# Both FFNs' end in a Trainium2 trunk layer: three tiles scaled between the last operands, the shift of four tiles moved to TensorE

## The reference, cut to what matters

```python
h = modulate(rms_normalize(x), sh1, sc1)              # h*(1+scale)+shift
x = x + 0.5 * gt1 * swiglu(h, w_ffn1_in, w_ffn1_out)  # first FFN, hidden 2816
h = modulate(rms_normalize(x), sh2, sc2)              # <- made at the end of the first FFN
y = hybrid_mixer(h, ...)
x = x + gt2 * y
h = modulate(rms_normalize(x), sh3, sc3)
x = x + 0.5 * gt3 * swiglu(h, w_ffn2_in, w_ffn2_out)  # second FFN
return rms_normalize(x) * g_final                     # <- made at the end of the second FFN
```

## Time and profile before

| | |
|---|---|
| median of 3 runs | 1986.99 us (1985.71 to 1988.73) |
| the profiled execution, its own time | 1988.55 us |
| its span in the profile, first to last instruction | 1986.8 us (1.75 us lie around it) |
| mean granted TensorE clock | 0.985 |
| end of the first FFN (last item to the barrier) | 705 to 735 us of the span |
| end of the second FFN | 1965 to 1987 us of the span |

### The profile page before, as it was taken

The page is one execution under the profiler, slowest core; times in us unless marked ns, Lnnn a source line. Parts: engine busy times, 40 slices in busy tenths (PEclk is TensorE's granted clock), DMA queues, the critical chain, the costliest instruction groups (busy, mean ns, idle before and its releaser), DMA issues. The chain is left out here.

```text
span 1986.8 us, 25496 instructions
## 1 busy us (share of the span) xinstructions
PE 1908.7 (96%) x9368; PEld 1568.6 (79%) x9368; DVE 1163.5 (59%) x1696; ACT 756.8 (38%) x1382; POOL 835.3 (42%) x612
## 2 busy tenths in 40 slices
PE   6989999999999989999999998998999999999997
PEld 6878888888888867777778887776888888888886
DVE  5876666654777771454514556568345344458777
ACT  4542223232444532554513444244333332334444
POOL 1597887674000111000011241398788778700002
PEclk7999999999999989999999999999999999999999
DMA  9155666633975300311112112513232233168652
GB/s 339 58 192 182 191 190 197 189 117 117 370 239 192 107 22 25 125 44 43 64 33 69 51 35 85 205 71 122 85 128 96 95 113 103 58 226 338 203 190 85
DMA packets 208107, 267.94 MB, mean 135 GB/s; under 512 B 14302, under 2 KB 125170, under 8 KB 206450
## 3 DMA queue, kind: packets, MB, share of 16 engines
q1 hardware_dynamic: 207986, 266.34, 40.0%
HBM read 211.16 MB, written 53.03 MB: 133 GB/s over the span
## 5 line engine op out<-in xcount | busy, mean ns | idle before, releaser
L446 POOL TENSOR_TENSOR ffn_ring_b<-ffn_raw_in,ffn_ring_b 128x512 fp32r<-128x512 f32 x156 | 222.9, 1437 | 113.6 <-ACT ffn_ring_b L441 113.6
L1052 PE MATMUL bank<-ffn_w_hi,ffn_a_hi 128*128 128x512 f32 x616 | 240.0, 390 | 1.2 <-DVE ffn_w_lo L1036 1.2
L1054 PE MATMUL bank<-ffn_w_hi,ffn_a_lo 128*128 128x512 f32 x616 | 239.7, 389 | 0.0
L1053 PE MATMUL bank<-ffn_w_lo,ffn_a_hi 128*128 128x512 f32 x616 | 239.6, 389 | 0.0
L1803 POOL TENSOR_TENSOR mx_w_lo<-mx_raw_w,mx_w_hi 128x1024 fp32r<-128x1024 f32 x26 | 62.7, 2421 | 357.5 <-ACT mx_w_hi L1606 290.7
L109 POOL TENSOR_SCALAR rms<-rms 128x1 f32<-128x1 f32 x24 | 13.3, 555 | 469.7 <-ACT ffn_junk L103 455.1
L441 ACT CAST ffn_ring_b<-ffn_raw_in 128x512 fp32r<-128x512 f32 x160 | 99.2, 622 | 267.4 <-PE bank L1504 255.6
L1025 ACT CAST ffn_a_hi<-ffn_a_stage 128x512 fp32r<-128x512 f32 x154 | 95.6, 621 | 200.4 <-PE bank L1054 196.0
L1319 DVE TENSOR_TENSOR ffn_u<-bank,ffn_u 128x512 f32<-128x512 f32 x106 | 72.9, 688 | 158.0 <-PE bank L1504 157.9
L1036 DVE TENSOR_TENSOR ffn_a_lo<-ffn_a_stage,ffn_a_hi 128x512 fp32r<-128x512 f32 x154 | 106.4, 691 | 73.6 <-ACT ffn_a_hi L1025 73.5
L446 POOL TENSOR_TENSOR ffn_ring_a_lo<-ffn_raw_in,ffn_ring_a_hi 128x512 fp32r<-128x512 f32 x96 | 132.2, 1388 | 31.9 <-ACT ffn_ring_a_hi L441 29.9
(11 more groups left out here) (379 smaller groups left out, 4750.2 us busy)
## 6 DMA issues: line engine op xcount, KB each, us to landing
ffn_raw_in<-in_w_ffn_in SPq DMA_DIRECT2D x88, 512.0 KB, 5.9
ffn_a_stage<-hidden SPq DMA_DIRECT2D x154, 256.0 KB, 3.7
ffn_w_stage<-in_w_ffn_out SPq DMA_DIRECT2D x132, 256.0 KB, 3.4
ada_rest<-in_w_ada SPq DMA_DIRECT2D x64, 448.0 KB, 3.9
hidden<-ffn_u SPq DMA_DIRECT2D x88, 256.0 KB, 2.0
hidden<-ffn_g SPq DMA_DIRECT2D x66, 256.0 KB, 2.0
mx_raw_w<-in_w_mix_in SPq DMA_DIRECT2D x28, 512.0 KB, 4.2
xres<-in_x SPq DMA_DIRECT2D x16, 512.0 KB, 8.7
```

What stands on the lines that cost most here:

```text
L446: pool.tensor_tensor(self.lo(q), self.source(b, m), self.hi(q).bitcast(F32), ALU.subtract)\
L1052: pe.matmul(dst, a_hi, w_hi, start=first, stop=False, skip_group_check=True)
L1053: pe.matmul(dst, a_hi, w_lo, start=False, stop=False, skip_group_check=True)
L1054: mm = pe.matmul(dst, a_lo, w_hi, start=False, stop=True, skip_group_check=True)
```

## The change

- In both FFNs ScalarE's `square` of tiles 0 to 3 comes after items 70 to 73 instead of 71 to 74.
- In both FFNs VectorE scales tiles 0, 1 and 2 between the items, behind items 72, 73 and 74, and tile 3 after the last item.
- First FFN: VectorE adds the shift to tiles 0 to 3 alone. Tiles 4 to 7 are transposed unshifted, and TensorE adds the shift in PSUM: for each of the two banks of a tile two more matmuls of 512 columns, with the shift's high and low part (4 rows of 128) as one operand and a 4 x 512 pattern of ones and zeros as the other. For that the shift is also loaded as rows (4 x 2 x 128); ScalarE makes their high part and the pattern behind item 70 (`rows_hi`), and VectorE their low part after the last item (`rows_lo`).
- First FFN: the 128 x 1024 shift has another place in memory, so its load moves from item 44 to a point after all items' loads, behind a wait for the low parts of item 68.
- Second FFN: `scale_out(4)` comes behind the last `add` instead of ahead of it.

```diff
@@ class Norm
+    def rows_hi(self, act):
+        act.wait_ge(self.loaded, 32)
+        act.copy(self.rows["hi"], self.rows["raw"]).then_inc(self.rows_done, 1)
+        act.copy(self.rows["name"], self.c.ident[0:4, 0:4].unsqueeze(2).to_broadcast([4, 4, P]))\
+            .then_inc(self.rows_done, 1)
+    def rows_lo(self, dve):
+        dve.wait_ge(self.rows_done, 2)
+        dve.tensor_tensor(self.rows["lo"], self.rows["raw"], self.rows["hi"].bitcast(F32), ALU.subtract)\
+            .then_inc(self.rows_done, 1)
@@ def turn(self, pe, t)
+        by_pe = self.rows and not on_dve
+        if by_pe:
+            pe.wait_ge(self.scaled, t + 1)
+            pe.wait_ge(self.rows_done, 3)
...
-                mm = pe.transpose(c.bank[:, self.bank_of(t) + half, k * P:(k + 1) * P],
-                                  self.xn[t][:, (4 * half + k) * P:(4 * half + k + 1) * P], c.ident[:, :])
+                mm = pe.matmul(bank[:, k * P:(k + 1) * P], self.xn[t][:, (4 * half + k) * P:(4 * half + k + 1) * P],
+                               c.ident[:, :], start=(k == 0), stop=(k == 3 and not by_pe), is_transpose=True,
+                               skip_group_check=True)
+            if by_pe:
+                names = self.rows["name"].rearrange("p b n -> p (b n)")
+                pe.matmul(bank, self.rows["hi"][:, half, :], names, start=False, stop=False, skip_group_check=True)
+                mm = pe.matmul(bank, self.rows["lo"][:, half, :], names, start=False, stop=True, skip_group_check=True)
@@ ffn()
-                (0, 1, 2, 3, 4, 5, 0, 1), dve_tiles=range(NS), all_dve=True)
+                (0, 1, 2, 3, 4, 5, 0, 1), dve_tiles=range(4), rows=buf.rows if next_mod is not None else None)
@@ sync
             if next_mod is not None:
+                sp.wait_ge(fo.lo_done, 2 * (len(fo.items) - fo.J + 3))
+                norm.load_shift(sp, next_mod)
                 sp.wait_ge(fo.lo_done, 2 * (len(fo.items) // fo.STAGES * fo.STAGES))
                 after.load(sp)
@@ scalar
-                if 71 <= n < 75:
-                    act.wait_ge(fo.added, fo.final(n - 71))
-                    norm.square(act, n - 71)
+                if n == 70 and next_mod is not None:
+                    norm.rows_hi(act)
+                if 70 <= n < 74:
+                    act.wait_ge(fo.added, fo.final(n - 70))
+                    norm.square(act, n - 70)
@@ vector
+                if 72 <= n < 75:
+                    if next_mod is None:
+                        scale_out(n - 72)
+                    else:
+                        norm.scale(dve, n - 72)
...
-            for t in range(4):
-                if next_mod is None:
-                    scale_out(t)
-                else:
-                    norm.scale(dve, t)
-                    if t == 1:
-                        dve.wait_ge(fo.lo_done, 2 * len(fo.items))
-                        after.cut_lo(dve)
+            if next_mod is not None:
+                norm.rows_lo(dve)
+                norm.scale(dve, 3)
+                dve.wait_ge(fo.lo_done, 2 * len(fo.items))
+                after.cut_lo(dve)
+            else:
+                scale_out(3)
             for t in range(NS + 2):
...
-                    if 3 <= t < 7:
-                        scale_out(t + 1)
+                    if 4 <= t < NS:
+                        scale_out(t)
```

More of the change, by code:

```diff
@@ L75, in __init__ @@
     def __init__(self, core, tag, shift, scale1, junk, xn, first_bank, places=None, dve_tiles=(5, 7),
-                 all_dve=False):
+                 rows=None):
         self.c, self.shift, self.scale1, self.junk, self.DVE_TILES = core, shift, scale1, junk, dve_tiles
@@ L80, in __init__ @@
         self.freed_by = [max([i for i in range(t) if places[i] == places[t]], default=None) for t in range(core.NS)]
-        self.first_bank = first_bank
+        self.first_bank, self.rows = first_bank, rows
         s = core.sem
@@ L87, in __init__ @@
         self.scaled = s(f"{tag}_scaled")
-        self.shifted = [None if all_dve else s(f"{tag}_shifted_pool"), s(f"{tag}_shifted_dve")]
+        self.shifted = [None if rows else s(f"{tag}_shifted_pool"), s(f"{tag}_shifted_dve")]
+        if rows:
+            self.rows_done, self.shift_loaded = s(f"{tag}_shift_rows_done"), s(f"{tag}_shift_loaded")
         self.turned = s(f"{tag}_turned")
@@ L93, in load, with load_shift @@
     def load(self, sp, m):
-        sp.dma_start(self.shift, self.c.mod(m)).then_inc(self.loaded, 16)
-        sp.dma_start(self.scale1, self.c.mod(m + 1)).then_inc(self.loaded, 16)
+        if self.rows:
+            D = self.c.D
+            sp.dma_start(self.rows["raw"], self.c.mod_rows[m * D:(m + 1) * D].rearrange("(h b f) -> b h f", h=2, f=P))\
+                .then_inc(self.loaded, 16)
+        else:
+            sp.dma_start(self.shift, self.c.mod(m)).then_inc(self.loaded, 16)
+        sp.dma_start(self.scale1, self.c.mod(m + 1)).then_inc(self.loaded, 16)
+    def load_shift(self, sp, m):
+        sp.dma_start(self.shift, self.c.mod(m)).then_inc(self.shift_loaded, 16)
+    def rows_hi(self, act):
[7 more added lines that the diff above has]
+            .then_inc(self.rows_done, 1)
     def bank_of(self, t):
@@ L124, in scale @@
         if t in self.DVE_TILES:
+            if self.rows:
+                dve.wait_ge(self.shift_loaded, 16)
             dve.wait_ge(self.scaled, t + 1)
@@ L138, in turn @@
         on_dve = t in self.DVE_TILES
-        pe.wait_ge(self.shifted[on_dve], sum((i in self.DVE_TILES) == on_dve for i in range(t + 1)))
+        by_pe = self.rows and not on_dve
[3 more added lines that the diff above has]
+        else:
+            pe.wait_ge(self.shifted[on_dve], sum((i in self.DVE_TILES) == on_dve for i in range(t + 1)))
         if t >= 2:
@@ L142, in turn @@
         for half in range(2):
+            bank = c.bank[:, self.bank_of(t) + half, :]
             for k in range(4):
-                mm = pe.transpose(c.bank[:, self.bank_of(t) + half, k * P:(k + 1) * P],
-                                  self.xn[t][:, (4 * half + k) * P:(4 * half + k + 1) * P], c.ident[:, :])
+                mm = pe.matmul(bank[:, k * P:(k + 1) * P], self.xn[t][:, (4 * half + k) * P:(4 * half + k + 1) * P],
[5 more added lines that the diff above has]
+                mm = pe.matmul(bank, self.rows["lo"][:, half, :], names, start=False, stop=True, skip_group_check=True)
             mm.then_inc(self.turned, 1)
@@ L488, in __init__ @@
         self.gate = c.at("ffn_gate", [P, D], c.GATE)
-        self.shift, self.scale1 = c.at("ffn_shift", [P, D], c.SHIFT), c.at("ffn_scale1", [P, D], c.SCALE1)
+        at = c.SHIFT
+        self.rows = {"raw": c.at("ffn_shift_raw", [4, 2, P], at)[:, :, :],
+                     "hi": c.at("ffn_shift_hi", [4, 2, P], at + 1, F32R)[:, :, :],
+                     "lo": c.at("ffn_shift_lo", [4, 2, P], at + 2, F32R)[:, :, :],
+                     "name": c.at("ffn_tile_name", [4, 4, P], at + 3, F32R)[:, :, :]}
+        self.shift, self.scale1 = c.at("ffn_shift", [P, D], c.T_LOW), c.at("ffn_scale1", [P, D], c.SCALE1)
         self.junk = c.at("ffn_junk", [P, D], c.JUNK)
@@ L1431, in _, with scale_out @@
                     start.dve_rest(dve, b, 7)
+            def scale_out(t):
+                if t == 0:
+                    dve.wait_ge(norm.loaded, 16)
+                dve.wait_ge(norm.rms_done, t + 1)
+                dve.scalar_tensor_tensor(core.xres[:, t, :], core.xres[:, t, :], core.rms[:, 2, t:t + 1],
+                                         buf.scale1[:, :], ALU.mult, ALU.mult).then_inc(norm.scaled, 1)
             for n in range(1, len(fo.items)):
```

## The result

The changed kernel takes 1992.0 us, the kernel before 1987.5 us when measured beside it (medians of 17 executions each). The ratio is 1.0019 with a 95% interval of 1.0012 to 1.0025, so the change costs 2.4 to 5.0 us. That is slower, and it lies on the edge of the 0.2% that the prediction counts as "the same": just under it by the ratio, just over it by the medians (4.5 us, 0.23%). The profiled execution took 1991.28 us with a span of 1989.5 us.

What follows compares the result with a forecast made beforehand. TensorE, busy 96% of the span, was taken as the bound. Early scales -1.1, TensorE's shift +3.9 and second FFN 0 gave +2.8 us on the profiled 1988.55, 1989.8 on the median; range 1984.8 to 1992.3.

Steps and rivals of the forecast that it cites:

- (a): Rival, 0.23: clock stays high in the shortened gap before `turn(2)`, giving back 2.6 us (1987.2); mixer gap up to 1.6 more.
- Part 1, gaps filled: First FFN: early scales and shifts fill VectorE's gaps before the last items, bringing the first `evict` 2.53 us earlier.
- Part 1, `rows_lo`: First FFN: making the shift's low part on VectorE adds 0.33 us before the first `evict`.
- Part 1, waits for GpSimd: First FFN: two of VectorE's scales wait for GpSimd's power, 0.55 us each, 1.10 us in all.
- rival (c): Rival, 0.10: GpSimd gets in only during VectorE's waits, on four scales, costing 3.7 us instead of 1.1: 1992.4.
- rival (b): Rival, 0.12: GpSimd gets in at the next border between VectorE instructions, no scale waits, 1.1 us less: 1988.7.
- Part 1, ScalarE, SyncE, items pushed back: First FFN: later low parts make TensorE stand up to 1.3 us; this, ScalarE's added copies and SyncE's later load cost nothing.
- Part 2, the price of the matmuls: First FFN's turns: 16 added 4-row matmuls at 0.23 us, 3.68 us, plus 0.54 for transpose changes; 4.2 us taken.
- Part 2, VectorE loses nothing on the path: First FFN: VectorE is spared four additions of some 1.2 us, behind 713.2 where TensorE is the bound, so gain nothing.
- Part 3: Second FFN's end: earlier scales are covered and the reordered scale 4 changes nothing, 0 us; bounds -0.7 and +0.8.
- Clock: First FFN: TensorE's wait before `turn(2)` shrinks to 3.7 us, clock still falls, so the 2.6 us loss stays.
- Rival (d): Rival, 0.06: scales wait as long as the gaps were, first `evict` stays at 708.6, TensorE's shift paid in full: 1990.9.

Runs made afterwards that it cites:

- e5: Changed kernel with VectorE shifting all tiles, no row operands and the second FFN's old order, leaving the first FFN's early scales and shifts; 1984.35 us, ratio 0.9988.
- e1: Changed kernel with the shift's operands on 128 rows, 124 of them zero, instead of 4; 1988.02 us, ratio 1.0001 to the kernel before.
- e2: Changed kernel with VectorE shifting all eight tiles again, row operands still made but unused; 1985.4 us, ratio 0.9990 to the kernel before.
- e8: e7 with TensorE shifting tiles 6 and 7 alone, by one matmul of 128 rows for each bank; 1984.3 us, ratio 0.9987 to the kernel before.
- e3: Changed kernel with the second FFN's last scales back in their old order, tile 4 ahead of the last addition; 1990.35 us, ratio 1.0015.
- e6: Changed kernel with high and low parts in one 128-row operand, one added matmul per bank instead of two, pattern made on GpSimd; 1986.66 us, ratio 0.9995.
- e7: e5 plus 12 matmuls with unused results between the turns of tiles 1 and 2, to fill TensorE's idle time; 1984.58 us, ratio 0.9987.

## Why the prediction was right or wrong

The forecast of +2.8 us to 1989.8 was 2.2 us below the median, inside the range, and of the right sign. 0.5 of the 2.2 is the kernel before, whose median was 1987.5 here and not 1987.0. (The range's lower end, 1984.8, doesn't follow from its words: (a) less all of the second gap's 1.6 is 1985.6.) Its sum for the profiled pair (+2.8 against 2.1 at the two places) came out near by luck, because terms that were wrong stood against each other:

| term | predicted | in the profiled pair |
|---|---|---|
| gaps filled, `rows_lo`, waits (first `evict` behind the stage's start) | -1.10 | -2.21 |
| TensorE's shift of four tiles | +4.2 | +6.5 |
| cover at its end | -0.3 | -0.6 |
| clock | 0 | -2.4 |
| second FFN | 0 | +0.8 |

The clock's term is the length from `turn(2)` to the next turn, with the same code in both: 6.09 us before (713.19 to 719.28), all but the last 1.0 us at the low clock, and 3.66 after (711.03 to 714.69). The cover is what is left of the turns: 25.88 - 22.36 = 6.5 - 2.4 - 0.6.

- **Part 1, gaps filled.** Right: e5, which has no `rows_lo`, has its first `evict` 2.51 us earlier in the stage, against 2.53 predicted.
- **Part 1, `rows_lo`.** Right: 0.33 us from start to start (701.37 to 701.70).
- **Part 1, waits for GpSimd.** Wrong, and the largest error of this part: two waits of 0.55 us priced, none found. The 3.58 us of the earlier trace rows was true, but I read it as "GpSimd gets in only when VectorE stands". The rows show otherwise: the power of 687.39 was done 0.3 us behind the border between the first scale and its shift, while VectorE ran on. I had named this border in rival (c) as an argument against that rival, and not used it on the forecast. But it isn't the only way in, and perhaps not needed: the power of 1958.16 ended 0.5 us behind the start of a scale (1960.95) that depends on no operation just before it. I also left out how much time GpSimd has: tile 1's inverse was done before the first scale, like tile 0's, and in the second FFN, without shifts, the same scales between the items had one wait of 0.44 us and not two. The end of my bounds without waits was the true one, and rival (b) had the right outcome. Its rule, from the Trainium skill's page "SBUF — State Buffer", section "SBUF: two separate sides", that whoever starts first holds the port for that whole instruction, is not what the rows show either: the power of 1964.17 took 4.48 us, over six VectorE operations. Both the hold and the way in are in the trace; what decides between them was not tried.
- **Part 1, ScalarE, SyncE, items pushed back.** Nearly right: TensorE's last item ends 0.55 us later in the stage, with one wait of 0.23 us, and it costs nothing.
- **Part 2, the price of the matmuls.** The step that failed was "so I take the 0.23 us from start to start" for a matmul of 4 rows between matmuls of 128. I had searched for the price by rows used, from 64-row matmuls that follow their own kind. What costs is the change of the row count: 0.33 us instead of 0.23 from the low part's matmul to what follows, and 0.53 to 0.58 instead of 0.35 for the four transposes ahead. With 128 rows my price was right to 0.05 us a tile (e1).
- **Part 2, VectorE loses nothing on the path.** Right for the kernel before and only by 0.24 us (22.4 against 22.1). Once `turn(2)` starts earlier and less of the turns runs at 1.2 GHz, VectorE becomes the bound (e2, e5), and two shifts fewer are worth something (e8).
- **Part 3.** The upper end of the bounds, +0.8, for the reason given there: tile 5's inverse is held until the end of scale 4. The step that failed was to let the gain of the earlier square and the hold cancel; e3 has the old order and the old 10.06 us.
- **Clock.** The wait became 3.2 us and not 3.7, since the waits for GpSimd didn't come (which makes it shorter) and TensorE's items ended 0.55 us later and not 1.2 (which makes it longer). Then the clock fell in some profiles and not in others; in the profiled execution rival (a) came true. Where it fell (e1, e3), it was low for 3.4 us of work (711.6 to 715.0 and 712.3 to 715.7) and not for the 5.1 of the earlier trace rows, so even then a third of the loss was gone. Rival (a)'s 2.6 us was right in size (2.4), but paid in a kernel whose TensorE work I had priced too low. Its second part, the gap before the mixer, did not come: TensorE stood 3.01 us there, and the clock was low from 736.8 to 740.2, as long as before.
- **Rival (d)** is out by the first `evict`. **Rival (c)** had the right total (1992.4) by the wrong mechanism: no scale waited.

## What to carry to other kernels

Price a small matmul by a row in which it stands between the matmuls that it will stand between: among matmuls of 128 rows, four rows cost more than 128 with zeros, and folding two into one saved another 0.45 us a tile, where making them small had cost 0.63. When work is moved from one engine to another, write down both engines' times for the stretch; here they lay 0.24 us apart, so moving four shifts overshot, and moving none or two gave the shortest times (1984.35 and 1984.3 us, which can't be told apart). Work that fills an engine's gaps costs nothing only with its inputs ready. Here they were: two inverses were done before the first scale, and the other two 7 us and more ahead of theirs.

## What the runs showed of the hardware

- A change of the row count between 128 and 4 on TensorE costs: turns of 2.43 us against 1.80 with 128 rows, with the weight load at the change starting with its matmul (PEld idle 0.17 and 0.36 us). Between two matmuls of 4 rows it costs nothing (0.33 us against 0.32).
- After a wait of 3.2 us the clock may be 1.2 or 2.4 GHz. It was low after 3.24, 3.25, 3.27 and 3.49 us (e2, e3, e1, e6), high after 3.21 and 2.91 us (changed, e5). It need not fall inside the wait: in e2, e1 and e3 it fell 0.5, 0.6 and 1.0 us behind the start of `turn(2)`. The waits of 2.34 us at `turn(7)` were both followed by a fall, in e7 0.1 us behind the turn's start, as this row of 1 us shows, and in e5 1.5 us behind it, when the turn was over. So the length of a wait alone doesn't tell whether the work behind it runs at the low clock.

```profile
729.00:730.00 1.00, 1.00 (x6) 0.50 0.00 0
```

- The same power of 128 x 1 elements on GpSimd takes 0.55 us when VectorE stands (1982.64), 1.47 us beside a scale and its shift (687.39), and 4.48 us beside six VectorE operations (1964.17).
